# A two-block model kernel: the first layer's way to its latent attention, rebuilt

## What is computed

```python
mod = silu(c) @ w_ada + b_ada                    # six quarters of shift, scale, gate
h = rms_norm(x, g_mix) * (1 + sc1) + sh1
q_lat, kv_lat, k_rope = split(h @ w_in)          # 256, 128 and 32 columns, then the rest
q_a = rms_norm(q_lat, g_q) @ w_uq                # 8 heads of 64 plain + 32 rotated columns
kv_n = rms_norm(kv_lat, g_kv)
k_nope, v_a = kv_n @ w_uk, kv_n @ w_uv           # 8 heads of 64
q = concat(q_a[:64], rope(q_a[64:], positions))
k = concat(k_nope, rope(k_rope, positions))      # one rotated key for all heads
o_a = softmax(q k^T / sqrt(96) + mask) v_a
```

## Time and profile before

| | us |
|---|---|
| median of three runs | 2206.35 |
| lowest and highest | 2202.04, 2209.09 |
| profiled execution, its own time | 2201.93 |
| its span | 2200.0 |
| PE busy | 2033.4 |
| DVE, ACT, POOL busy | 1027.1, 638.8, 163.0 |
| mean granted clock of PE | 0.951 of full |

### The profile page before, as it was taken

How to read it: one execution, slowest core, us unless ns; L and a number is a source line. 1 busy time by engine, 2 the same in 40 slices (tenths; PEclk the granted TensorE clock), 3 DMA queues, 4 the chain that set the end, 5 groups by cost and what they waited for, 6 DMA issues and landing times.

```text
span 2200.0 us, 23508 instructions
## 1 busy us (share of the span) xinstructions
PE 2033.4 (92%) x8878; PEld 1350.6 (61%) x8878; DVE 1027.1 (47%) x1872; ACT 638.8 (29%) x1201; POOL 163.0 (7%) x168
## 2 busy tenths in 40 slices
PE   6798998995799997997899999999989999999998
PEld 3246765763333332544578888885645877888886
DVE  6356463344211111867655555553113757554554
ACT  3155351223111111334532222220013644222222
POOL 2000000002111111211210000002000001000001
PEclk8899999997799998897999999999998999999999
DMA  9411503444599877320122323222251012232211
GB/s 328 153 39 34 196 11 143 167 180 172 204 418 364 343 290 295 144 74 1 39 77 77 115 78 114 84 108 77 77 198 39 1 37 78 85 107 94 98 39 39
DMA packets 103143, 286.84 MB, mean 130 GB/s; under 512 B 13156, under 2 KB 24106, under 8 KB 89986
## 3 DMA queue, kind: packets, MB, share of 16 engines
q1 hardware_dynamic: 91360, 266.24, 32.9%
q0 software_dynamic: 10048, 16.81, 2.2%
q10 hardware_dynamic: 1634, 2.43, 0.3%
HBM read 329.43 MB, written 21.01 MB: 159 GB/s over the span
## 4 chain that ended last, share of the span: by engine, by line
PE 84%; DVE 7%; DMA 3%; ACT 3%; issue 2%; POOL 1%; SPq 0%; ACTq 0%; DVEq 0%; POOLq 0%
PE bank L1259 14%; PE bank L1260 14%; PE bank L1261 14%; PE bank L1163 13%; PE bank L1586 8%; PE bank L1612 4%; PE bank L1218 3%; DMA weight_ring<-in_w_ada 2%; PE bank L1230 2%; PE bank L1244 1%; PE bank L1772 1%; PE bank L1570 1%; PE bank L1454 1%; PE bank L1250 1%; POOL chunk_mask L1026 1%
## 5 line engine op out<-in xcount | busy, mean ns | idle before, releaser
L1261 PE MATMUL bank<-hidden_high,weights_low 128*128 128x512 f32 x896 | 351.5, 392 | 0.0
L1259 PE MATMUL bank<-hidden_high,weights_high 128*128 128x512 f32 x704 | 276.9, 393 | 11.9 <-DVE weights_low L2500 5.3
L2848 DVE TENSOR_TENSOR weights_low<-weight_ring,weights_high 128x1024 fp32r<-128x1024 f32 x128 | 161.3, 1260 | 269.6 <-ACT weights_high L2051 269.6
L1260 PE MATMUL bank<-hidden_low,weights_high 128*128 128x512 f32 x640 | 249.9, 391 | 0.0
L2051 ACT ACTIVATE weights_high<-weight_ring 128x1024 fp32r<-128x1024 f32 x128 | 135.6, 1060 | 324.2 <-PE bank L1261 324.2
L1259 PE MATMUL bank<-normed_high,weights_high 128*128 128x512 f32 x512 | 201.5, 394 | 3.9 <-DVE weights_low L2848 3.9
L1260 PE MATMUL bank<-normed_low,weights_high 128*128 128x512 f32 x512 | 200.6, 392 | 0.0
L1261 PE MATMUL bank<-normed_high,weights_low 128*128 128x512 f32 x512 | 200.5, 392 | 0.0
L1163 PE MATMUL bank<-arena,weight_ring 128*128 128x512 f32 (+3 forms) x436 | 196.0, 605 | 3.9 <-DVE arena L2412 3.9
L1955 ACT ACTIVATE arena<-bank 128x512 f32<-128x512 f32 (+7 forms) x273 | 129.7, 489 | 228.5 <-PE bank L1163 107.5
L1261 PEld LDWEIGHTS bank<-hidden_high,weights_low 128*128 128x128 f32 x896 | 170.0, 190 | 35.9
(11 more groups left out here) (441 smaller groups left out, 3124.6 us busy)
## 6 DMA issues: line engine op xcount, KB each, us to landing
weight_ring<-in_w_up SPq DMA_DIRECT2D x16, 2048.0 KB, 8.6
weight_ring<-in_w_down SPq DMA_DIRECT2D x16, 2048.0 KB, 7.9
weight_ring<-in_w_gate SPq DMA_DIRECT2D x29, 1024.0 KB
weight_ring<-in_w_up SPq DMA_DIRECT2D x29, 1024.0 KB
weight_ring<-in_w_ada SPq DMA_DIRECT2D x12, 2048.0 KB, 12.5
weight_ring<-in_w_down SPq DMA_DIRECT2D x19, 1024.0 KB
toeplitz_bias<-in_w_down SPq DMA_DIRECT2D x19, 1024.0 KB
weight_ring<-in_w_in SPq DMA_DIRECT2D x7, 2048.0 KB, 12.7
```

Source lines behind the costliest of these rows:

```text
L1259: pe.matmul(dst, high, rhs_high, start=first, stop=False)
L1260: pe.matmul(dst, high, rhs_low, start=False, stop=False)
L1261: return pe.matmul(dst, low, rhs_high, start=False, stop=last)
L2848: dve.tensor_tensor(piece_half(w_lo, ch, q), piece_of(ch, q), piece_half(w_hi, ch, q).bitcast(F32), ALU.subtract).then_inc(s_wlo, 1)
```

## The change

The setup (`small_setup`) comes ahead of the transposition of x on PE, and the small inputs' DMAs are reordered on ACT; positions, frequencies and the rotation matrix are loaded for all 128 partitions (nine DMAs in place of three). The squares of x are summed by eight PE matmuls. PE takes four, three, two and two of the eight products of the four modulation rows, DVE the rest. DVE multiplies x by the reciprocal root, ACT applies scale and shift. The weights of the latents are loaded third. The latents' first four products run between the two halves of the modulation, the last four after them. The shared key's eight matmuls write four quarters of the output partitions, and are added up by a matmul that also copies the 32 rows four times (`k_fold`), once plain and once rotated. The latents are used with their gains but without their norm: the sums of squares are made as columns (`lat_sums`), the reciprocal roots are spread by two matmuls with diagonals (`lat_roots`), and are multiplied into the rotation tables and the key latent. Each query head has 128 weight columns: 64 plain, 32 to rotate and the same 32 rotated, laid out by ACT; one DVE product by a table of ones, cosines and sines follows. Keys are laid out in the same way with 128 rows, and made two heads at a time. GpSimd's table is read into place after the last query group.

```diff
 MOD_FIRST = (2, 0, 3, 1)
+MOD_PE = (4, 3, 2, 2)
+MOD_DONE = tuple(sum(KD - k for k in MOD_PE[:n + 1]) for n in range(len(MOD_PE)))
...
-        chunk(("ada", c))
-        if n == 1:
...
     group("pos")
     group("toe2", 2)
     group("table_T")
     group("toe1")
-    group("lat", 4)
-    chunk("in_lat")
...
+    group("tp_x", KD)
+    group("vec")
+    group("norm_mix")
+    for pair in (MOD_FIRST[0:2], MOD_FIRST[2:4]):
+        for c in pair:
+            group(("mod_sum", c))
+        for c in pair:
+            group(("mod", c))
+    group("lat", 3)
+    group("kr")
+    for c in MOD_FIRST:
+        chunk(("ada", c), last=G[("mod_sum", c)])
+        if c == MOD_FIRST[1]:
+            chunk("in_lat", last=G["kr"])
+    group("lat_sums")
+    group("k_fold", 2)
+    group(("uq", 0))
+    group(("uq", 1))
+    group("lat_roots", 2)
+    for h in range(2, H):
         group(("uq", h))
-    for h in range(H):
-        group(("rot", h))
-    group("uk", H)
+    group("uk", H // 2)
     group("uv", NT)
     chunk("mla_w", 3)
...
+            w_in = a["w_in"][0]
             for c in MOD_FIRST:
                 put_ada(c)
-            w_in = a["w_in"][0]
-            put("in_lat", [(0, kt(w_in, 0, 416))])
+                if c == MOD_FIRST[1]:
+                    put("in_lat", [(0, kt(w_in, 0, 416))])
...
+            for table, rows in ((rope_even, slice(0, 64)), (rope_odd, slice(64, 128))):
+                link(pool.memset(table[rows, :], 1.0))
+            link(pool.memset(fold4[:, :], 0.0))
+            for n in range(7):
+                link(pool.affine_select(out=fold4[:, :].rearrange("p (a b) -> p a b", a=4),
+                                        in_=fold4[:, :].rearrange("p (a b) -> p a b", a=4), compare_op=ALU.not_equal,
+                                        fill=1.0, base=32 * (n - 3), pattern=[[0, 4], [-1, 32]], channel_multiplier=1))
+            pool.wait_ge(s_angle, 16 * 9)
+            pool.tensor_copy(rot4[:, :].rearrange("p (a b) -> p a b", a=4),
+                             rot[:, :].unsqueeze(1).broadcast_to([P, 4, ROPE])).then_inc(s_fold, 1)
             pool.wait_ge(s_rv, 16)
             pool.dma_start(toe_dram, bass.AP(rv_dram.tensor, 127, [[TOEW, H], [-1, P], [1, T]]))\
                 .then_inc(s_toe, 16)
             pool.wait_ge(s_toe, 16)
+            pool.wait_ge(s_rv2, 16)
+            pool.wait_ge(mm_done, done(G[("uq", H - 1)]))
...
+            small_setup()
+            for j in range(KD):
+                begin(G["tp_x"] + j)
+            for t in range(NT):
+                pe.wait_ge(s_x[t], 16)
+                for j in range(KD):
+                    last = pe.transpose(psum(G["tp_x"] + j)[:, t * P:t * P + P], x_tok[:, t, j * P:j * P + P],
+                                        ident[:, :])
+                    if t == NT - 1:
+                        last.then_inc(mm_done, 1)
...
+            def norm_mix():
+                g = G["norm_mix"]
+                begin(g)
+                for j in range(KD):
+                    pe.wait_ge(s_sq, j + 1)
+                    last = pe.matmul(psum(g)[:, :], ones[:, :], hT[:, j, :], start=(j == 0), stop=(j == KD - 1))
+                last.then_inc(mm_done, 1)
...
+            mod_row_sum(MOD_FIRST[0], 0, norm_mix)
+            mod_row_sum(MOD_FIRST[1], 1)
+            for n in range(2):
+                mod_row_turn(MOD_FIRST[n], n)
...
+            def latents(half):
                 for m in range(3):
+                    if not half:
...
+            latents(0)
+            mod_row_sum(MOD_FIRST[2], 2)
+            mod_row_sum(MOD_FIRST[3], 3)
+            for n in range(2, 4):
+                mod_row_turn(MOD_FIRST[n], n)
+            latents(1)
+            g = G["kr"]
+            begin(g)
+            for half in range(2):
+                for c in range(4):
+                    last = pe.matmul(psum(g)[32 * c:32 * c + 32, :], w[:, 4 * half + c, 384:416],
+                                     hT[:, 4 * half + c, :], start=(half == 0), stop=(half == 1),
+                                     skip_group_check=True)
+            last.then_inc(mm_done, 1)
+            pe.wait_ge(s_lsq, 3)
+            g = G["lat_sums"]
+            begin(g)
+            for n, tiles in enumerate(((0, 1), (2,))):
+                for t in range(NT):
+                    last = tile(g, psum(g)[:, NT * n + t:NT * n + t + 1],
+                                [(lat_sq[:, m, t * P:t * P + P], ones[:, 0:1]) for m in tiles], fresh=False)
+            last.then_inc(mm_done, 1)
+            g_read(pe, G["kr"])
+            pe.wait_ge(s_fold, 1)
+            for n, table in enumerate((fold4, rot4)):
+                g = G["k_fold"] + n
+                tile(g, psum(g)[:, :], [(table[:, :], kr_parts)]).then_inc(mm_done, 1)
             c = W["mla_w"]
             w_ready(pe, c)
...
+            w_uk, w_uv = ws(c, (1, 512), 1536), ws(c, (1, 512), 2048)
+            pe.wait_ge(s_uqw, 1)
...
+            def query_up(h):
                 g = G[("uq", h)]
-                tile(g, psum(g)[0:QK, :], [(w_uq[:, k, h * QK:h * QK + QK], q_lat_n[:, k, :]) for k in range(2)])\
+                w_q = (w_uq_even, w_uq_odd)[h % 2]
+                tile(g, psum(g)[:, :], [(w_q[:, k, h // 2, :], q_lat_g[:, k, :]) for k in range(2)])\
                     .then_inc(mm_done, 1)
-            for h in range(H):
-                g = G[("rot", h)]
...
+            query_up(0)
+            query_up(1)
+            pe.wait_ge(s_diag, 1)
+            for n in range(2):
+                g = G["lat_roots"] + n
+                tile(g, psum(g)[:, :], [(ones[:, :], root_diag[:, n, :])]).then_inc(mm_done, 1)
+            for h in range(2, H):
+                query_up(h)
+            pe.wait_ge(s_kvn, 1)
+            for p in range(H // 2):
+                g = G["uk"] + p
+                tile(g, psum(g)[:, :], [(w_uk[:, 0, p * P:p * P + P], kv_lat_n)]).then_inc(mm_done, 1)
...
+            act.dma_start(sbuf_s[:, 0, :].bitcast(I32), bass.AP(a["positions"].tensor, 0, [[0, P], [1, T]]))\
+                .then_inc(s_angle, 16)
+            for n in range(4):
+                act.dma_start(inv_freq[32 * n:32 * n + 32, :], a["inv_freq"]).then_inc(s_angle, 16)
+                act.dma_start(rot[32 * n:32 * n + 32, :], a["rotate"]).then_inc(s_angle, 16)
...
+            for rows, table, arg in ((slice(0, P), rope_cos, rope_cos_arg), (slice(0, P), rope_sin, rope_sin_arg),
+                                     (slice(64, 96), rope_even, rope_cos_arg),
+                                     (slice(96, 128), rope_even, rope_sin_arg),
+                                     (slice(0, 32), rope_odd, rope_cos_arg),
+                                     (slice(32, 64), rope_odd, rope_sin_arg)):
+                act.activation(table[rows, :], arg[rows, :], ACT.Sin).then_inc(s_trig, 1)
...
+            def modulated(half):
+                act.wait_ge(s_mod1, half + 1)
+                for j in range(4 * half, 4 * half + 4):
+                    act.wait_ge(s_unit, j + 1)
+                    act.activation(hT[:, j, :], hT[:, j, :], ACT.Identity, scale=scale1[:, j:j + 1],
+                                   bias=modT[:, j:j + 1]).then_inc(s_h, 1)
+            g_read(act, G["norm_mix"])
+            act.activation(rtmp[:, :], rtmp[:, :], ACT.Sqrt).then_inc(s_std, 1)
+            mod_row_out(0)
+            mod_row_out(1)
+            modulated(0)
+            mod_row_out(2)
+            c = W["mla_w"]
+            w_ready(act, c)
+            w_uq = ws(c, (2, 768)).rearrange("p k (h two c) -> p k h two c", h=H // 2, two=2)
+            even, odd = w_uq[:, :, :, 0, :], w_uq[:, :, :, 1, :]
+            act.activation(w_uq_even[:, :, :, 0:96], even, ACT.Copy)
+            act.activation(w_uq_even[:, :, :, 96:112], even[:, :, :, 80:96], ACT.Copy, scale=-1.0)
...
+            act.activation(w_uq_odd[:, :, :, 48:64], odd[:, :, :, 64:80], ACT.Copy).then_inc(s_uqw, 1)
+            mod_row_out(3)
+            modulated(1)
             g = G["lat"]
             for m in range(3):
-                evac(g + m, lat_raw[:, m, :])
-            evac(g + 3, kr_raw[64:96, :], psum(g + 3)[64:96, :])
...
+                act.wait_ge(mm_done, done(g + m))
+                act.activation(lat_sq[:, m, :], psum(g + m)[:, :], ACT.Square).then_inc(s_lsq, 1)
+                evac(g + m, q_lat_g[:, m, :] if m < 2 else kv_lat_n, scale=col("g_q", m) if m < 2 else col("g_kv"))
+            evac(G["kr"], kr_parts)
+            act.wait_ge(s_lsum, 1)
+            act.activation(lat_root[:, :, :], lat_root[:, :, :], ACT.Sqrt).then_inc(s_lroot, 1)
+            act.wait_ge(s_kr, 1)
+            for n, r in enumerate((slice(64, 128), slice(0, 64))):
+                act.activation(k_mla.rearrange("p (h two) t -> p h two t", two=2)[r, :, n, :],
+                               k_cos[r, :].unsqueeze(1).broadcast_to([64, H // 2, T]), ACT.Copy).then_inc(s_rotd, 1)
+            for p in range(H // 2):
+                g = G["uk"] + p
```

(82 more changed lines are left out.)

275 lines of the change are left out of this document (85 added, 190 removed).

## The result

The changed kernel takes 2176.13 us, the median of four runs (2174.54 to 2177.61); the kernel before, beside it, 2206.95 us (2202.04 to 2209.09, four runs). The ratio is 0.9851 with an interval of 0.9829 to 0.9873. Forecast were 2177 us, with a range of 2168 to 2190. The profiled execution took 2175.25 us, its span 2173.2 us, at a mean granted clock of 0.956; for the kernel before these were 2201.93, 2200.0 and 0.951.

The account below looks back on a forecast made before the run. PE was taken as the bound, with 84% of the chain. The rebuilt front's terms put the attention's start at 109.7 us instead of 139.2; 29.5 us off the median 2206.35 gave 2177, range 2168 to 2190.

Parts of the forecast that it names:

- The reckoning by the attention's start: First attention's scores start at 109.7 us instead of 139.2; everything later shifts along by 29.5 us.
- Setup first: Front of kernel: six more ACT issues at 0.44 us, x's transpositions from 18.7 us, first row sum done at 27.8.
- Both turns are covered: First modulation half: both row turns end near 41.3 us, under the reciprocal chain, so latents start at 43.1.
- Latents in halves: Two halves of 10.3 us around the second modulation, whose last row copy waits for ACT's seven layout copies until about 59.9.
- Shared key: After the latents: 16 instructions into four output quarters take 4.1 us instead of 7.00; bounds 1.8 and 7.0.
- Norms and rotations: Before the attention: norm work of 18 us leaves the path, and sixteen rotation instructions leave PE's 36.95 us stretch.
- Tail: Just ahead of the first attention's scores: last copy and wait take 1.1 us.
- Clock: One half-clock start charged before each latents half, 2 x 2.5 us, moving the attention's start from 104.7 to 109.7.
- The table: GpSimd's Toeplitz table, read in after the last query, is there by about 110 us, before the second attention wants it.
- more cold stretches: Rival: two to four more half-clock stretches before the attention, 2.5 to 3.3 us each, giving 2184 us; chance 0.14.
- The late quarter: Rival: last modulation quarter's weights land near 60 us, DVE starts 9 us late, giving 2186 us; chance 0.12.
- The half clock all along: Rival: clock stays at half along the whole new front, some 68 us more, giving 2240 us; chance 0.04.

Follow-up runs that it names:

- after_again: The changed kernel run once more, unaltered, in more rounds: 2177.45 us, ratio 0.9871 to the kernel before.
- x_first: Against the changed kernel, x is transposed ahead of the setup and DVE copies out all eight tiles of x: 2170.34 us, ratio 0.9835.

## Why the prediction was right, step by step

- **The reckoning by the attention's start held.** 109.7 forecast, 110.53 and 108.99 measured; 29.5 us of shift forecast, 28.7 there; 2176.9 forecast, 2176.13 measured. Everything behind the scores shifted along, the wait for weights at 213.64 too. That the median fits to 1 us is partly luck: errors of 1 to 3 us cancelled ahead of the scores, and the shift was 26.8 us at the end of the profiled execution, while the medians moved by 30.8 here and by 28.8 beside after_again.
- **Setup first** was costed 1.4 to 3 us too low. The six further issues weren't 0.44 each: two rows of the trace show 0.64 and 1.01. And the first row sum waits for a copy of x (25.75, 1.30), which I had left out: row sum one ends at 30.78, not 27.8. That this order delays x was right; x_first puts about 6 us on it.
- **"Both turns are covered" failed, by a tenth of a microsecond.** The chain goes through the second row's turns, which end at 44.11 (42.22 + 1.89), then the addition, the scale and ACT's first product: 45.55, not 43.1. DVE was done with the reciprocal at 42.69 and with the first two products at 44.01, so the reciprocal would have held the latents almost as long. Both were late by 2 to 3 us (reckoned: turns 41.3, reciprocal 40.5), because PE's first row sum ended 3.0 late.
- **Latents in halves.** Second half at 66.50 where 65.2 was reckoned. The seven layout copies hardly matter: between the third and the fourth row's turns PE waits a tenth of a microsecond.
- **Shared key**: 1.85, my lower bound, where I took 4.1. The nearest row, narrow products of 128 columns, was the wrong one to lean on: with products of 512 columns two quarters gave 6.98 / 3.56, or 2.0 times, and four gave 3.8.
- **Norms and rotations**: the mechanisms are right, and shown by leaving them out (16.8 and 9.5 us). The 18 us reckoned for the norms was the whole stretch; leaving the norms out freed 16.8. These are prices in the kernel before.
- **Tail**: 1.1 reckoned, 1.35 measured from PE's last product, so this term held. ACT's two long copies of the key took 1.92 each, as reckoned, but end at 92.07 and not near 88; they are still under the queries, as ACT then waits for PE until 103.2.
- **Clock**: 5.0 charged for two starts; 3.7 measured for these (24.45 less 20.80), and a third of about 1.7 behind the sums, 5.3 in all. In after_again it is 4.7 (25.49 less 20.80) and no third. The total held; the places didn't.
- **The table**: GpSimd's next step on it, which waits for the read, starts at 112.5, about the forecast 110, and the chain has no wait for it.

Of the rivals, more cold stretches came in part (one more in one of two executions, not two to four). The late quarter didn't come: DVE's partials ran on, and the engines were idle (9 GB/s) from 50 us. The half clock all along didn't come either: 1.00 from 50 to 52 and from 57.7 to 63 us. Nor did small inputs hold the set-up until 44 us: its last products start at 18.02.

What stays open: what brings the clock down ahead of each half of the latents, why the half-clock spots lie elsewhere from one execution to the next, and what the set-up would cost in its old place.

## What to carry to other kernels

When a change rebuilds a whole front, reckon one date, the start of the first stage that needs all of it, and check each station on the way: here the total was right while half of its parts were off. Ask of each part alone which side it falls on; the set-up ahead of x cost about 6 us inside a change that won 31. And where the chain leaves an engine, look up that engine's own last instruction before calling the rest a wait: of the 3.05 us at the tail, 1.7 were products of PE, and an experiment aimed at a gap that was hardly there.

## What the runs showed of the hardware

- Products into different quarters of a bank's partitions ran side by side whatever their order in the program: 16 instructions took 6.98, 3.56 and 1.85 us with one, two and four quarters in use.
- The granted clock fell to half behind 24 one-column products through which PE was busy without a gap (2.70 of 2.70 us, then 0.53), and in two other executions, of after_again and x_first, it stayed at 1.00 behind the same products. Full-width fillers put straight ahead of the latents saved nothing.
- Two executions of the same kernel had their half-clock spots in different places, and the scores 1.5 us apart.
- 31 small DMAs on ACT's queue take until 14.97 us to issue, at 0.26 to 1.01 us each, and ACT computes nothing before. With 15 of them behind x and 2 MB of weights in SP's queue, the last vector landed 8.25 us after its issue, where small loads on ACT's queue took 5.6 to 6.6.
